# Layer 0's attention: values of two parts as weights, probabilities scaled on GpSimd and moved as high and low parts

## What is computed

```python
probs = jax.nn.softmax(logits, axis=-1).astype(v.dtype)
out = jnp.einsum('btcgk,btkcd->btcgd', probs, v_sel)
```

## Time and profile before

| | |
|---|---|
| median of 3 runs | 3264.56 us (3256.2 to 3266.32) |
| the profiled execution | 3254.72 us, span 3252.9 us |
| TensorE, busy share of the span | 95% |
| VectorE, ScalarE, GpSimd | 47%, 27%, 31% |
| granted TensorE clock, mean | 0.973 of 2.4 GHz |

### The profile page before, as it was taken

The page is one execution under the profiler, slowest core; times in us unless marked ns, Lnnn a source line. Parts: engine busy times, 40 slices in busy tenths (PEclk is TensorE's granted clock), DMA queues, the critical chain, the costliest instruction groups (busy, mean ns, idle before and its releaser), DMA issues.

```text
span 3252.9 us, 49145 instructions
## 1 busy us (share of the span) xinstructions
PE 3091.2 (95%) x19621; PEld 2890.8 (89%) x19621; DVE 1544.2 (47%) x2890; ACT 883.0 (27%) x1919; POOL 1021.4 (31%) x495
## 2 busy tenths in 40 slices
PE   8896999989999999999989999998999999999996
PEld 8586777778999999999988999976899999999996
DVE  1699765444543333433364555465454333343335
ACT  2456544433001111001033455453401011100112
POOL 2132000035444333334233222213444343333432
PEclk9998899989999999999999999999999999999998
DMA  2121000012211111111012111111222111111101
GB/s 86 40 50 49 1 1 1 1 64 70 87 55 46 51 45 45 45 39 52 13 59 58 50 50 47 44 40 59 75 77 65 39 52 45 50 47 39 50 2 54
DMA packets 209373, 149.75 MB, mean 46 GB/s; under 512 B 28915, under 2 KB 195765, under 8 KB 209237
## 3 DMA queue, kind: packets, MB, share of 16 engines
q1 hardware_dynamic: 209236, 147.85, 15.3%
HBM read 128.09 MB, written 19.73 MB: 45 GB/s over the span
## 4 chain that ended last, share of the span: by engine, by line
PE 88%; DVE 7%; issue 2%; ACT 2%; POOL 1%; DMA 1%; SPq 0%; POOLq 0%; ACTq 0%; DVEq 0%
PE psum L153 48%; PE psum L2054 16%; PE psum L1658 6%; PE psum L625 4%; PE psum L591 2%; PE psum L606 2%; DVE junk L840 2%; PE psum L1246 2%; PE psum L1220 2%; PE psum L1234 1%; PE psum L546 1%; PE psum L560 1%; PE psum L1195 0%; PE psum L1612 0%; PE psum L1857 0%
## 5 line engine op out<-in xcount | busy, mean ns | idle before, releaser
L153 PE MATMUL psum<-x_hi,w_hi 128*128 128x352 f32 (+1 forms) x3192 | 1041.7, 326 | 25.3 <-DVE gate L2291 15.3
L153 PE MATMUL psum<-x_lo,w_hi 128*128 128x352 f32 (+1 forms) x3192 | 1028.2, 322 | 0.0
L153 PE MATMUL psum<-x_hi,w_lo 128*128 128x352 f32 (+1 forms) x3192 | 1028.1, 322 | 0.0
L122 POOL TENSOR_TENSOR w_hi<-w_raw,zeros 128x1024 fp32r<-128x1024 f32 (+1 forms) x209 | 381.8, 1827 | 1531.4 <-PE psum L153 952.8
L153 PEld LDWEIGHTS psum<-x_hi,w_hi 128*128 128x128 f32 (+1 forms) x3192 | 601.8, 189 | 28.0 <-issue 27.2
L153 PEld LDWEIGHTS psum<-x_lo,w_hi 128*128 128x128 f32 (+1 forms) x3192 | 603.1, 189 | 0.5
L153 PEld LDWEIGHTS psum<-x_hi,w_lo 128*128 128x128 f32 (+1 forms) x3192 | 601.6, 188 | 0.5
L124 POOL TENSOR_TENSOR w_lo<-w_raw,w_hi 128x1024 fp32r<-128x1024 f32 (+1 forms) x209 | 491.2, 2350 | 16.4
L2307 DVE TENSOR_TENSOR gate<-psum,gate 128x352 f32<-128x352 f32 x120 | 63.0, 525 | 750.2 <-PE psum L153 750.2
L2054 PE MATMUL psum<-h_hi,w_hi 128*128 128x352 f32 x1056 | 340.8, 323 | 1.2 <-DVE h_lo L2329 1.0
L2054 PE MATMUL psum<-h_lo,w_hi 128*128 128x352 f32 x1056 | 338.3, 320 | 0.0
(11 more groups left out here) (461 smaller groups left out, 4124.6 us busy)
## 6 DMA issues: line engine op xcount, KB each, us to landing
w_raw<-in_ffn_w_dram SPq DMA_DIRECT2D x132, 512.0 KB
w_raw<-in_b_w_in_dram SPq DMA_DIRECT2D x24, 512.0 KB
w_raw<-in_ple_w_gate_dram SPq DMA_DIRECT2D x16, 512.0 KB
x_nat<-in_x_prompt_dram SPq DMA_DIRECT2D x8, 512.0 KB, 8.2
w_raw<-in_a_w_in_dram SPq DMA_DIRECT2D x8, 512.0 KB
w_raw<-in_a_w_in_dram SPq DMA_DIRECT2D x16, 256.0 KB
x_rows<-x_rows SPq DMA_DIRECT2D x8, 512.0 KB, 2.6
out_new_b_v_prompt_dram<-valsB SPq DMA_DIRECT2D x8, 512.0 KB, 3.3
```

Of the source, the lines that this page charges most:

```text
L122: nc.gpsimd.tensor_tensor(c.w_hi[s][:, 0:kc], c.w_raw[s][:, 0:kc], zero, ALU.add).then_inc(c.split[s], 1)
L153: last = c.nc.tensor.matmul(out, w, x, start=(n == 0), stop=(n == 3 * len(terms) - 1))
```

## The change

The probabilities are now normalised before they are transposed: `exps` accumulates the row sum, VectorE inverts it (`invert`), and GpSimd multiplies the row by it (`scale_probs`). The transposed groups are split: ScalarE copies each to `pt_hi` (`high`), VectorE subtracts that from PSUM into `pt_lo` (`low`). The next group for the same bank waits for the subtraction. The values are split likewise once, high and low parts side by side in one weight block of 128 columns (`v_split`), in the memory of `x_hi` and `x_lo`. A product has this block as weights, and the 256 columns of two heads move, once from `pt_hi`, once from `pt_lo`. Rows 0 to 63 of the result are the sums with the high values, rows 64 to 127 those with the low ones. ScalarE copies the lower rows to SBUF (`take_low`), VectorE adds the two (`add_parts`) straight into `c.o_col`. Column of ones, `scale_outputs`, `turn_outputs` and `take_output` go.

```diff
-    vals = c.at("valsA", [P, VBLK, KV, 65], F32, A_BLOCKS["vals"])
+    vals = c.at("valsA", [P, VBLK, KV, 64], F32, A_BLOCKS["vals"])
...
+    v_split = [spare[0][:, 0:VBLK], spare[0][:, VBLK:2 * VBLK], spare[0][:, 2 * VBLK:3 * VBLK], spare[1][:, 0:VBLK]]
...
+        def scale_probs(step, m):
+            t, sl = step // 8, step % 3
+            L, n = keys_of(t), height(t)
+            g.wait_ge(s_inv, 2 * step + m + 1)
+            nc.gpsimd.tensor_scalar(prob[0:n, sl, m, 0:L], prob[0:n, sl, m, 0:L],
+                                    inverse[0:n, 2 * sl + m:2 * sl + m + 1], None, ALU.mult).then_inc(s_prob, 1)
...
+        values_low(0)
+        values_low(1)
+        for step in range(STEPS):
+            scale_probs(step, 0)
+            scale_probs(step, 1)
+            if step in (0, 1):
+                values_low(2 + step)
...
-            pe.wait_ge(s_exp, 2 * g + m + 1)
+            pe.wait_ge(s_prob, 2 * g + m + 1)
             if seq >= 2:
-                pe.wait_ge(s_pv, seq - 1)
+                pe.wait_ge(s_plo, seq - 1)
...
+        def multiply(grp, m, j):
+            t, c2, _, _ = heads(2 * grp)
+            n, gs, kv = height(t), groups(t), 2 * c2 + m
+            pe.wait_ge(s_plo, turned_all(2 * grp + 1, m, j))
...
+            out = bank(c, 6 + grp % 2).rearrange("p (m i q) -> p m i q", m=2, i=2)[:, m, :, 0:n]
             for x, blk in enumerate(gs[j]):
+                b, size = 4 * j + x, NEW if blk == VNEW else P
+                for pt in (pt_hi, pt_lo):
+                    mm = nc.tensor.matmul(out, v_split[kv][0:size, blk, :], pt[0:size, m, b, :, 0:n],
...
         for g in range(STEPS + 3):
+            turning = 2 <= g < STEPS + 2
+            if turning:
+                for k in turns_of(g - 2, 0):
+                    turn_over(g - 2, k)
             if g < STEPS:
                 logits(g)
+            second = list(turns_of(g - 2, 1)) if turning else []
+            if g % 2 == 0:
+                grp = (g - 4) // 2
...
+                for j in range(2):
+                    if j < parts:
+                        multiply(grp, 1, j)
+                    if j < len(second):
+                        turn_over(g - 2, second[j])
+            else:
+                grp = (g - 3) // 2
...
+                for j in range(2):
+                    if j < len(second):
+                        turn_over(g - 2, second[j])
+                    if j < parts:
+                        multiply(grp, 0, j)
```

ScalarE's loop, and VectorE's:

```diff
+        for g in range(STEPS + 4):
+            turning = 2 <= g < STEPS + 2
+            if turning:
+                for k in turns_of(g - 2, 0):
+                    high(g - 2, k)
             if 1 <= g <= STEPS:
                 exps(g - 1, 1)
+            if turning:
+                for k in turns_of(g - 2, 1):
+                    high(g - 2, k)
+            if g % 2 == 1 and g >= 5:
+                take_low((g - 5) // 2)
             if g < STEPS:
                 exps(g, 0)
+            if g in (0, 1):
+                values_high(2 + g)
...
+            if turning:
+                for k in turns_of(g - 2, 0):
+                    low(g - 2, k)
+            if 1 <= g <= STEPS:
+                invert(g - 1, 1)
+            if g % 2 == 1 and g >= 5:
+                add_parts((g - 5) // 2)
+            second = list(turns_of(g - 2, 1)) if turning else []
             if g < STEPS:
                 read_logits(g, 0)
+            for k in second[0:1]:
+                low(g - 2, k)
             if g < STEPS:
                 read_logits(g, 1)
+            for k in second[1:]:
+                low(g - 2, k)
+            if g < STEPS:
+                invert(g, 0)
                 for _ in itertools.islice(later, 2):
                     pass
```

More of the change, by code:

```diff
@@ L608, in turn_over @@
             mm.then_inc(s_tr, 1)
[L610 to L619, removed]
+        def multiply(grp, m, j):
+            t, c2, _, _ = heads(2 * grp)
+            n, gs, kv = height(t), groups(t), 2 * c2 + m
+            pe.wait_ge(s_plo, turned_all(2 * grp + 1, m, j))
+            if grp < 4:
+                pe.wait_ge(s_vlo, kv + 1)
+            if m == 0 and j == 0 and grp >= 2:
                 pe.wait_ge(s_oe, grp - 1)
-            gs = groups(t)
-            at = 512 * (6 + grp % 2) + 65 * (2 * m + i)
+            out = bank(c, 6 + grp % 2).rearrange("p (m i q) -> p m i q", m=2, i=2)[:, m, :, 0:n]
             for x, blk in enumerate(gs[j]):
[L624 to L636, removed]
+                b, size = 4 * j + x, NEW if blk == VNEW else P
+                for pt in (pt_hi, pt_lo):
+                    mm = nc.tensor.matmul(out, v_split[kv][0:size, blk, :], pt[0:size, m, b, :, 0:n],
+                                          start=(b == 0 and pt is pt_hi),
+                                          stop=(j == len(gs) - 1 and x == len(gs[j]) - 1 and pt is pt_lo))
+            if j == len(gs) - 1:
+                mm.then_inc(s_pv, 1)
         for i in range(len(pairs)):
@@ L646, in tensor @@
         for g in range(STEPS + 3):
-            n = len(turns(g - 2)) if 2 <= g < STEPS + 2 else 0
-            for k in range(min(2, n)):
-                turn_over(g - 2, k)
+            turning = 2 <= g < STEPS + 2
+            if turning:
+                for k in turns_of(g - 2, 0):
+                    turn_over(g - 2, k)
             if g < STEPS:
                 logits(g)
[L652 to L657, removed]
+            second = list(turns_of(g - 2, 1)) if turning else []
+            if g % 2 == 0:
+                grp = (g - 4) // 2
+                parts = len(groups(grp // 4)) if grp >= 0 else 0
+                for j in range(2):
[5 more added lines that the diff above has]
+                grp = (g - 3) // 2
+                parts = len(groups(grp // 4)) if grp >= 0 else 0
+                for j in range(2):
[3 more added lines that the diff above has]
+                        multiply(grp, 0, j)
     def scalar(act):
@@ L685, in rows @@
             else:
+                act.wait_ge(s_ones, 1)
                 ins = nc.scalar.activation(vals[0:NEW, VNEW, 2 * x:2 * x + 2, 0:64],
@@ L750, in scalar @@
                 after(sub)
[L751 to L754, removed]
+        act.wait_ge(s_cache, 32)
+        act.wait_ge(s_ones, 1)
+        values_high(0)
+        values_high(1)
+        for g in range(STEPS + 4):
[3 more added lines that the diff above has]
+                    high(g - 2, k)
             if 1 <= g <= STEPS:
                 exps(g - 1, 1)
-            if n > 2:
-                copy_turned(g - 2, 2)
+            if turning:
[3 more added lines that the diff above has]
+                take_low((g - 5) // 2)
             if g < STEPS:
                 exps(g, 0)
-            if g >= 4 and g % 2 == 0:
-                take_output((g - 4) // 2)
+            if g in (0, 1):
+                values_high(2 + g)
     def vector(v):
@@ new lines, in invert, with add_parts @@
+        def invert(g, m):
+            n, at = height(g // 8), 2 * (g % 3) + m
+            v.wait_ge(s_exp, 2 * g + m + 1)
+            nc.vector.reciprocal(inverse[0:n, at:at + 1], total[0:n, at:at + 1]).then_inc(s_inv, 1)
+        def add_parts(grp):
+            t, c2, j, _ = heads(2 * grp)
+            n = height(t)
+            v.wait_ge(s_low, grp + 1)
+            o = bank(c, 6 + grp % 2).rearrange("p (m i q) -> p m i q", m=2, i=2)
+            lo = low_part[0:64, grp % 2].rearrange("p (m i q) -> p m i q", m=2, i=2)
+            for i in (0, 1):
+                dst = c.o_col[64 * i:64 * i + 64, 4 * c2:4 * c2 + 4, P * t:P * t + n].rearrange("p (m j) q -> p m j q", j=2)
+                ins = nc.vector.tensor_tensor(dst[:, :, j], o[0:64, :, i, 0:n], lo[:, :, i, 0:n], ALU.add)
+            ins.then_inc(s_oe, 1)
@@ L976, in vector @@
         later = ()
-        for g in range(STEPS + 3):
+        for g in range(STEPS + 4):
             if g % 8 == 0 and g < STEPS:
```

93 lines of the change are left out of this document (46 added, 47 removed).

## The result

The changed kernel takes 3383.36 us, the median of four runs (3381.3 to 3385.4); the kernel before, beside it on the same chip, 3265.44 us (3256.2 to 3266.59). The ratio is 1.0362, with a 95% interval from 1.0339 to 1.0385: slower by 3.6%, 118 us. The profiled execution has a span of 3380.1 us, against the earlier trace rows: 127.2 us more, not 118, because the profiled execution of the kernel before, 3254.72 us, lies 10.7 us under the median of its runs.

A forecast was written before the change was run, and what follows sets the result against it. TensorE was taken to bound the loop. To 3254.7 us were added 47 (chain), 27 and 30 (clock, tiles 4 to 7 and 1 to 3), 5 (VectorE beside GpSimd), 3 (setup), less 10 for slack: 3357, stated 3358; range 3275 to 3420.

The forecast's parts named there:

- case (a): The forecast itself, layer 0 attention loop: serial chain over three engines, clock partly down, 3330 to 3390 us, chance 0.48.
- A: Start of a step's chain: the moment VectorE has subtracted the last group of the step before.
- (1): Odd step of tile 7: one group of four blocks turned on TensorE, 0.5 us after A.
- (6): Odd step of tile 7: ScalarE's copy of the high part, 0.5 us.
- (8): Odd step of tile 7: VectorE's two additions, ordered ahead of the read of logits, 0.75 us.
- (7): Odd step of tile 7: ScalarE's copy of the low rows, queued behind the high part, 0.6 us.
- The chain's sum: Longer steps through the serial chain at full clock, all tiles of the loop: 47 us more.
- The clock in tiles 4 to 7: One fall to half speed per pair of steps, 3.3 us long, 1.65 us lost each: 27 us.
- VectorE beside GpSimd: Later tiles' mask instructions on VectorE, delayed by GpSimd now running beside them: 5 us.
- Case (b): Attention loop: serial chain, clock nearly always full, 3302 us, with 3280 to 3325; chance 0.26.
- (c): Attention loop: clock down throughout, each chain growing by its TensorE terms, 3440 us; chance 0.10.
- Case (d): Odd steps: additions don't hold up the reads, as the low-row copy finds ScalarE free early; 3215 us, chance 0.12.

The follow-up runs named there:

- e1: Changed kernel with ScalarE's low-row copy ahead of head 1's high parts and VectorE's additions after the step's last subtraction: 3263.41 us, ratio 1.0007.
- e3: Changed kernel with only VectorE's additions moved behind the step's last subtraction, ScalarE's order kept: 3263.09 us, ratio 1.0007.
- e4: Changed kernel, order kept, with unread extra TensorE products after the last value products of odd steps in tiles 4 to 7: 3357.01 us, ratio 1.0297.
- e12: e4 plus six more unread products at the end of each step of tiles 0 to 3, from the fifth on: 3343.91 us, ratio 1.0237.
- e5: Changed kernel without GpSimd's scalings, TensorE waiting for the reciprocal instead, outputs unnormalised: 3375.27 us, ratio 1.0344.
- e6: e1 with head 1's first half of value products, in even steps, ahead of the second turned group and the logits: 3256.59 us, ratio 0.9975.
- e8: e6 with 40 unread TensorE products ahead of the attention loop: 3257.26 us, ratio 0.9975.
- e9: The kernel before the change with 40 unread TensorE products ahead of its attention loop: 3265.76 us, ratio 0.9994.
- e10: e8 with six more unread products at the end of each step of tiles 0 to 3: 3253.92 us, ratio 0.9966.

## Why the prediction was right, and where its sizes were off

The time forecast, 3358 us, is 25 us below the measured 3383.4; the range and the sign held, and the mechanism of case (a) is the one that the runs show: the serial chain over three engines, and a clock that is partly down. That the sum came so near is in part luck, as its two large terms were off in opposite directions. Of its signs VectorE's largest wait held. The busy time, the distances of the reads, the clock in tiles 1 to 3 and GpSimd under half busy (it was busy 251 of the 463 us from 322 to 785, 54%) did not.

**TensorE.** The new products have the pitch that I took, 0.12 us (693.30 to 693.41). But its busy time in the loop fell by 15 us only (327.5 us from 321 to 666 before, 312.8 from 322 to 785 after), not by over 60, mostly because its clock there is 0.79 on average where it was 0.94: in e1, at 0.97 over tiles 4 to 7, TensorE is busy 163 us in them, against 204 in the kernel before.

**The chain of an odd step.** It has the twelve pieces in the order forecast. From 690.07 (A) to 700.47 it is 10.4 us against 9.9: (1) 0.69 for 0.5, (6) 0.62 for 0.5, (8) 0.87 for 0.75, the rest within 0.07. e1 to e3 show that (7) and (8) are the cause: 120 us hang on the order of two small steps.

**The chain's sum, mis-sized.** Of the 67.5 us that tiles 4 to 7 lost, some 29 are the clock (the estimate from e4), and 38 the chain, forecast at 20. With 0.35 us taken off for each us at half clock, the steps of tiles 4 to 7 come to 6.6, 7.7, 8.3 and 8.8 us against my 6.2, 6.95, 7.7 and 8.5. The pieces were timed on tile 7; "the same sums with the shorter forms" came out 0.3 to 0.8 us short in each tile. In tiles 0 to 3 the chain is worth 32 us for 24. This term, 44 us of the sum for tiles 0 to 7, measured about 70, is the largest error. Which pieces grow in tiles 4 to 6 I did not trace. The sample tile, 6.5 us for 3, was not taken apart either.

**The clock in tiles 4 to 7.** It falls where I said, but the single fall in tile 7 is longer, 7 us (0.74 in the us from 699, 0.84 in that from 706) where one fall in the earlier trace rows gave me 3.3, and it lies over the turned group, the logits and the value products: 1.16, 3.71 and 1.49 us, against 0.69, 1.92 and 1.03 in the odd step, 2.7 us lost and not 1.65. The term still came out at 29 us for 27, because most of the others are shorter: windows of 1 us show 17 falls in the 16 pairs of tiles 4 to 7, some of 3 to 4 us and some near 7, and 84 us at half clock are 5.3 per pair. Reads of logits at alternate distances did appear, but as 8.6 and 11.9 us, not near 7 and 10. The Trainium skill, "TensorE: Matmul & The Clock Gate", section on the PE-mode transpose, says that transpositions don't count as activity for the gate. The stretch fits that and does not test it: between the last value product, over by 695.7, and the fall in the us from 699 TensorE ran one turned group alone, 0.63 us from 698.87, and was idle for the rest. The 10 us that I took off for slack had no ground.

**Tiles 0 to 3.** The clock stays down longer than before, but not through tiles 1 to 3 as I let it. One window for each of the three:

```profile
346.70:378.00 31.30, 19.84 (x88) 12.10 (x89) 21.59 (x82) 16.49 (x52) 15.06 (x16) 0.71 0.00 1
378.00:418.60 40.60, 27.63 (x120) 16.96 (x120) 29.87 (x92) 19.86 (x52) 21.93 (x18) 0.72 0.00 1
418.60:463.90 45.30, 29.50 (x156) 19.51 (x157) 32.04 (x82) 23.30 (x52) 25.44 (x16) 0.88 0.00 1
```

And it is worth about 12 us (e12), not 30: with a clock of 0.93 the four tiles took 130 us for 142. These 18 us too many made up for most of the 26 by which the chain's term was short.

**GpSimd.** A scaling of 128x1024 takes 2.84 us, outside my bounds of 1.0 to 2.4: a row with one operand fewer is not a lower price. It stays hidden in the changed kernel, where GpSimd waits 211 us for reciprocals; in e1 it costs 5 us. **The step that was wrong** is "The tail is as long as before. The DMAs are the same." I did not ask what stands behind the scalings in GpSimd's queue: two weight splits of the next phase, 9.3 us, and a load behind them. That cost 6 us. No run put the splits ahead of the scalings with these kept, so that repair was not tried.

**VectorE beside GpSimd.** Forecast 5 us. The instructions of the masks did take about 6 us more in all, but the loop was not longer by it: in e5 3 us of the 6 are gone, and its tiles take 422.2 us like those of the changed kernel. So no run shows a price in time for this term, and what it measures is near nothing. Two rows of the masks in the changed kernel that grew:

```profile
L953 DVE TENSOR_TENSOR_SCAN rankA<-tieA 128x1024 int16<-128x1024 bf16 x1 | 2.8, 2809 | 0.0
...
L947 DVE TENSOR_SCALAR tieA<-bias 128x384 bf16<-128x384 f32 x1 | 1.6, 1579 | 0.0
```

Before, the same two took 2.29 and 0.35 us. For the second the timeline of the changed kernel shows what ran beside it, the subtraction of the values:

```profile
325.01 1.54 POOL L549 TENSOR_TENSOR x_hi<-valsA,x_hi 128x640 fp32r<-128x640 f32 x1
325.18 1.58 DVE L947 TENSOR_SCALAR tieA<-bias 128x384 bf16<-128x384 f32 x1
```

It ends with GpSimd's instruction. In e5, where GpSimd pauses from 325.23 to 325.65, the same instruction takes 0.38 us from 325.06. It has one SBUF input, so my condition "many with two SBUF inputs" was too narrow; the Trainium skill, "SBUF — State Buffer", Who interferes with whom, counts `tensor_scalar` among the operations that can take the shared pair, and this agrees.

**The rivals.** Case (b), clock nearly full, at 3302, and (c), clock down throughout, at 3440, are out by the windows: the mean over tiles 4 to 7 is 0.85. Case (d) was put at 3215, and e1 and e3 are that case made real: additions that hold up nothing. They give 3263, 48 us more. Tiles 4 to 7 gain 12 us there (200.7 against 213.1), where I had 1 to 1.9 us a step, 32 to 61 us; tiles 0 to 3 lose 18 where I said even, and the projection 6. In e1 VectorE's reads and subtractions still alternate with TensorE's work: of its chain of waits from 435 to 635 us TensorE carries 39% and VectorE 42%. So without the waits for the additions the change only breaks even, and the 72 us of value products that left TensorE bought nothing until e6's further step.

## What to carry to other kernels

When work leaves the bounding engine and comes back as short steps on three others, write out the order in which each queue serves them, and price every step that stands ahead of the one that frees the bound: a copy of 0.6 us and additions of 0.85 us, each cheap, cost 120 us by their places. An engine that was idle in a stretch may have been working ahead for the next phase; what is put into its queue pushes that work behind. A share of the chain of waits says who ended last, not what would be gained: 30% of it fell away in one run, and the stretch was as long as before.

## What the runs showed of the hardware

- A us at half clock cost 0.35 us over tiles 4 to 7 (estimated from e4 against the changed kernel), and in one fall in tile 7 2.7 us were lost in 7, where the fall lay over the logits. Products put ahead of the gaps took the time at half clock from 84 to 31 us and did not end the falls.
- Products ahead of the loop did not hold the clock in it: after 40 of them it was at 0.50 for 20 us (330 to 350) in e8 and till about 375 us in e9. Six per step inside the small tiles hold it at 0.98 from 330 to 440 us (e10).
- GpSimd multiplies 128x1024 float32 by one number per row in 2.84 us, and 128x128 in 0.65 us; its addition of two operands of 128x1024 takes 1.91 us.
